# A hybrid encoder step with a mixture of experts on one core: the order of the loads around the last stage

## What is computed

```python
def finish_layer(x, p, o_attn, c, lp):
    ...
    x = x + mixed
    h = rms_norm(x, lp['g_ffn']).reshape(B * T, D)
    idx, wts = hier_route(h, lp['w_coarse'], lp['b_coarse'], lp['w_fine'], lp['b_fine'])
    x = x + moe_ffn(h, idx, wts, lp['w_e_gate'], lp['w_e_up'], lp['w_e_down']).reshape(B, T, D)
    gate = jax.nn.sigmoid(rms_norm(x, lp['g_ple']) @ lp['w_ple_gate'])
    return x + gate * (p @ lp['w_ple_proj'])
```

## Time and profile before

| | |
|---|---|
| median of three runs | 1413.82 us |
| profiled execution | 1412.76 us |
| its span in the profile | 1410.5 us |
| TensorE matmul, busy | 1283.0 us (91%) |
| VectorE, busy | 957.3 us (68%) |
| ScalarE, busy | 718.7 us (51%) |
| GpSimd, busy | 398.6 us (28%) |
| chain that ended last, by engine | PE 70%, DVE 11%, DMA 4%, issue 2% |
| last block's last scatter issued | 1255.82 us |
| first expert rows issued | 1260.67 us |
| last output issued | 1407.15 us |

### The profile page before, as it was taken

One profiled execution on the slowest core, in us unless ns is written; L12 is line 12 of the kernel. 1 busy time (PEld: TensorE's weight loads), 2 busy tenths in 40 slices (PEclk: granted clock), 3 DMA queues, 4 the chain that ended last, 5 costly groups with the idle time before them and its releaser, 6 DMA issues.

```text
span 1410.5 us, 18160 instructions
## 1 busy us (share of the span) xinstructions
PE 1283.0 (91%) x6337; PEld 1067.9 (76%) x6337; DVE 957.3 (68%) x940; ACT 718.7 (51%) x872; POOL 398.6 (28%) x399
## 2 busy tenths in 40 slices
PE   5999878889888799987999999999999999948887
PEld 4888867777676688845788888888888888837765
DVE  4233845655566332275999999999999999965443
ACT  4224034545453221241877777777777777742121
POOL 1000023443402000003344444444444444420000
PEclk9999989989858899988999999999999999978999
DMA  7521002000004321126899999999999999953332
GB/s 264 128 59 31 1 16 90 16 25 1 15 22 151 125 90 60 45 98 248 319 396 379 378 377 372 372 380 378 384 393 390 398 400 398 379 217 116 119 105 75
DMA packets 72223, 289.54 MB, mean 205 GB/s; under 512 B 24048, under 2 KB 26800, under 8 KB 46830
## 3 DMA queue, kind: packets, MB, share of 16 engines
q1 hardware_dynamic: 61950, 271.03, 51.3%
q0 software_dynamic: 10224, 17.85, 3.3%
HBM read 276.13 MB, written 32.17 MB: 219 GB/s over the span
## 4 chain that ended last, share of the span: by engine, by line
PE 70%; DVE 11%; DMA 4%; issue 2%; ACT 2%; POOL 1%; SPq 0%; POOLq 0%; DVEq 0%; ACTq 0%
PE ps L419 18%; PE ps L421 18%; PE ps L420 18%; PE ps L1729 3%; PE ps L1848 3%; DMA mem<-y_rows 2%; PE ps L1736 2%; PE ps L1875 1%; PE ps L1860 1%; PE ps L1996 1%; DVE whl L408 1%; PE ps L1909 1%; PE ps L1810 1%; PE ps L2015 1%; DVE mem L1334 1%
## 5 line engine op out<-in xcount | busy, mean ns | idle before, releaser
L408 DVE TENSOR_TENSOR whl<-mem,whl 128x2048 fp32r<-128x2048 f32 (+2 forms) x219 | 491.4, 2248 | 30.9 <-ACT whl L1114 20.8
L419 PE MATMUL ps<-whl,ahl 128*128 128x512 f32 x1120 | 449.0, 401 | 6.4 <-DVE ahl L408 3.4
L420 PE MATMUL ps<-whl,ahl 128*128 128x512 f32 x1120 | 437.0, 390 | 0.0
L421 PE MATMUL ps<-whl,ahl 128*128 128x512 f32 x1120 | 436.9, 390 | 0.0
L1114 ACT ACTIVATE whl<-mem 128x2048 fp32r<-128x2048 f32 x202 | 387.3, 1919 | 96.0 <-PE ps L421 96.0
L419 PEld LDWEIGHTS ps<-whl,ahl 128*128 128x128 f32 x1120 | 217.9, 195 | 47.8 <-issue 4.8
L421 PEld LDWEIGHTS ps<-whl,ahl 128*128 128x128 f32 x1120 | 215.4, 192 | 44.4
L420 PEld LDWEIGHTS ps<-whl,ahl 128*128 128x128 f32 x1120 | 216.8, 194 | 40.0
L819 POOL DMA_INDIRECT y_rows<-mem x35 | 94.0, 2686 | 293.3 <-DVE mem L1630 292.5
L716 POOL TENSOR_SCALAR mem<-mem 128x1 f32<-128x1 f32 (+2 forms) x68 | 16.3, 240 | 514.2 <-ACT mem L893 411.3
L893 ACT ACTIVATE mem<-mem 128x1024 bf16<-128x1024 f32 (+1 forms) x54 | 49.2, 912 | 215.8 <-DVE mem L1463 100.2
(11 more groups left out here) (231 smaller groups left out, 1451.5 us busy)
## 6 DMA issues: line engine op xcount, KB each, us to landing
mem<-in_w_e_up SPq DMA_DIRECT2D x66, 1024.0 KB, 7.3
mem<-in_w_e_gate SPq DMA_DIRECT2D x66, 1024.0 KB, 7.3
mem<-in_w_e_down SPq DMA_DIRECT2D x66, 1024.0 KB, 7.7
mem<-in_x_prompt SPq DMA_DIRECT2D x24, 512.0 KB, 3.5
mem<-y_rows SPq DMA_DIRECT2D x16, 512.0 KB, 6.0
mem<-in_w_in SPq DMA_DIRECT2D x4, 1024.0 KB, 11.5
mem<-in_w_out SPq DMA_DIRECT2D x4, 1024.0 KB, 5.1
h_rows<-mem SPq DMA_DIRECT2D x8, 512.0 KB, 2.6
```

The lines of the kernel that those rows point to most:

```text
L408: return which.tensor_tensor(out, full, hi.bitcast(F32), ALU.subtract)
L419: nc.tensor.matmul(out, act_hi, whl[:, 0, w_at], start=first, stop=False)
L420: nc.tensor.matmul(out, act_hi, whl[:, 1, w_at], start=False, stop=False)
L421: return nc.tensor.matmul(out, act_lo, whl[:, 0, w_at], start=False, stop=last)
```

## The change

The norm vector gets a place of its own, over constants that are used up once the slot tables are made, and SyncE issues its load right behind its loop over the experts. The loads of the expert rows become a function; tiles 0 and 1 are issued ahead of the loop, and turn t of the loop issues tile t+2 in front of the gate rows and the output. The first three pairs each wait for the one low part that frees their buffer, in place of all four; the wait for all four goes to VectorE, in front of its first add. In the two loops over the gate-weight chunks, the last block's scaling moves from in front of chunk 3 to in front of chunk 2.

```diff
@@ -206,7 +206,7 @@
-        gple = xs[0]
+        gple = mem[:, P:P + D]
@@ -647,6 +647,7 @@
             sp.wait_ge(s_tab, 1)
+            sp.dma_start(gple, a["g_ple"][0].partition_broadcast(P)).then_inc(s_gm, 16)
             spilled = sp.value_load(ebk[0:1, 0:1].bitcast(I32), min_val=0, max_val=NE - 1)
@@ -680,17 +681,21 @@
             sp.wait_ge(s_moe, 1)
-            sp.wait_ge(s_mlv, J_PLE + 4)
-
+
+            def load_experts(t):
+                r = rows_of(t)
+                if t >= 3:
+                    sp.wait_ge(s_x2, t - 2)
+                else:
+                    sp.wait_ge(s_mlv, J_PLE + t + 1)
+                for k in range(2):
+                    sp.dma_start(yb[t % 3][k][0:r], Y[k * TOKENS + t * P:k * TOKENS + t * P + r]).then_inc(s_y[t % 3], 16)
+
+            load_experts(0)
+            load_experts(1)
             for t in range(NT + 3):
-                if t < NT:
-                    r = rows_of(t)
-                    if t >= 3:
-                        sp.wait_ge(s_x2, t - 2)
-                    for k in range(2):
-                        sp.dma_start(yb[t % 3][k][0:r], Y[k * TOKENS + t * P:k * TOKENS + t * P + r]).then_inc(s_y[t % 3], 16)
-                    if t == 0:
-                        sp.dma_start(gple, a["g_ple"][0].partition_broadcast(P)).then_inc(s_gm, 16)
+                if t + 2 < NT:
+                    load_experts(t + 2)
                 if 3 <= t <= NT:
                     load_projected(t - 1)
@@ -1168,7 +1173,7 @@
             for c in range(4):
-                if c == 3:
+                if c == 2:
                     out_left(0, J_PLE, 16 * (NE + 2), 2 * NE + 4)
                 expert_hi(None, c, c, 16 * (NE + 2), J_PLE + c - 3)
@@ -1704,6 +1709,7 @@
+            dve.wait_ge(s_mlv, J_PLE + 4)
             add_experts(0)
             x2_norm(0)
```

## The result

The changed kernel takes 1389.21 us, median of four runs (1388.53 to 1389.54), against 1413.21 for the kernel before in the same measurements; the ratio is 0.9833, with a 95% interval of 0.9821 to 0.9845. The forecast was 1391, its range 1387.5 to 1396. The profiled execution took 1388.99 us (span 1386.8), 23.8 less than that of before.

A forecast was written before the change was run, and what follows sets the result against it. The last stage was taken as bound by expert-row loads issued too late, TensorE next. 1412.76 - 19.16 (rows) - 3.56 (head) = 1390.04, plus 1.06 from profiled execution to median, gave 1391; range 1387.5 to 1396.

The forecast's parts named there:

- Rows two tiles ahead: Last stage: rows issued ahead of the output of tile t-3 end the load wait; turns 16.33 to 11.805, -19.16 us.
- The new wait on s_x2: On SyncE, ahead of gate rows and outputs: already over when SyncE comes to it.
- The first rival: Last stage: half the mean wait for rows stays, turn 13.2, time 1401; chance 0.08.
- The ring of VectorE and ScalarE: Last stage: their own turn of 10.1 us is a floor, 1.7 us a turn remaining before it takes over.
- The norm vector: Head of the last stage: with its load off the chain, the first add starts 1.66 us sooner.
- The cover in the expert loop: Scatter has 3.1 us cover against the vector's 1.66; cost taken as 0. Rival, loop delayed: 1392.7 to 1394.5, chance 0.09.
- The scaling: Last block's end: right half scaled at about 1252.3 instead of 1254.2, -1.9 us.
- all behind it moves with it: Behind the scaling: scatter, its 3.54 us to landing, GpSimd's word and SyncE's issue all move by the same 1.9 us.
- the forecast of the head: Start of the last stage: moves forward by 1.66 + 1.9 = 3.56 us, or 2.3 to 4.9 by the skill's clock rule.
- the wait for the fourth low part: Moved from SyncE to VectorE: waits for VectorE's own earlier work, so costs nothing.
- rows still just in time: Rival: SyncE held at some wait, only the head's 3.56 remains, time 1410; chance 0.04.
- a clock that stays low: Rival: TensorE's clock stays at its lower level through the last stage, about 1449 us; chance 0.03.

The follow-up runs named there:

- after: The changed kernel with all parts of the change, against the kernel before: 1389.21 us, ratio 0.9833.
- one_ahead: Against the changed kernel, expert rows loaded one tile ahead of the other transfers in place of two: 1388.44 us, ratio 0.9823.
- after_again: The changed kernel as it is, measured again on the same chip as the version with matmuls in both TensorE gaps: 1389.32 us, ratio 0.9827.
- after_busy_vector: Against the changed kernel, one more unread low part on VectorE right behind the right half's scaling: 1391.09 us, ratio 0.9841.
- scale_and_waits: Against the kernel before, scaling in front of chunk 2 and the changed kernel's split low-part waits: 1410.09 us, ratio 0.9976.
- norm_only: Against the kernel before, only the norm vector's own place and its load behind SyncE's expert loop: 1412.22 us, ratio 0.9996.
- scale_only: Against the kernel before, only the last block's scaling moved in front of chunk 2: 1412.61 us, ratio 0.9996.
- before: The kernel before the change, unaltered: 1413.21 us in the same measurements as the changed kernel.
- rows_only: Of the change only the expert rows' load order and its waits; norm vector and scaling as in the kernel before: 1394.03 us, ratio 0.9867.
- the run in which it idled 0.29 us ahead of the first transposes and 1.93 behind them: Against the changed kernel, 68 unread matmuls on TensorE between the last block and last stage: 1386.91 us, ratio 0.9815.
- the other run: Against the changed kernel, GpSimd's early read of the further-block count, 67 unread matmuls before the first transposes and 7 behind: 1386.20 us, ratio 0.9808.
- the run with early reading and without the second set: Against the changed kernel, 68 unread matmuls before the last stage, and GpSimd reads the further-block count during its last scatter: 1386.28 us, ratio 0.9814.

## Why the prediction was right, and where not

**Rows two tiles ahead: right to the tenth.** 19.16 was forecast, 112.88 - 93.68 = 19.20 came, and the run with that part alone shows it as its own. What is late next is TensorE, as said: turns of 11.80 at a clock of 1.00. The new wait on s_x2 cost nothing that shows there. The first rival, rows hidden only in part, found no place: even one tile of lead hides them. The ring of VectorE and ScalarE, 10.1 by the forecast, never took over.

**The norm vector: 1.66 forecast.** From the scatter's landing to the first add it took 7.93 us before (1255.82 + 3.54 to 1267.29 of the chain) and 6.36 after (1257.39 to 1263.75): 1.57. The cover in the expert loop held, at a cost of nothing (573.8 us before and after). That the same 16 engines run all DMAs and interleave them, as the Trainium skill says ("DMA: Bandwidth & Descriptors", section "Issuing engines are not separate DMA queues"), agrees with the vector's own landing: 8.6 us in the loop, beside the weights, 5.75 before. But nothing on the path had so little slack. One reading was a little off: the first add for tile 1 came 5.99 us after that for tile 0, not 5.8, which changes nothing.

**The scaling: 1.9 forecast, 1.90 came, and its landing was mis-sized.** From the left scaling to the scatter's issue it took 3.54 us before and 1.64 after. The step "all behind it moves with it: scatter, its 3.54 us to landing" took the landing for a constant. It fell by 1.17, to 2.37, because GpSimd issued the scatter beside an idle VectorE; the runs with the scaling alone and with VectorE kept at work show that as the cause. This is most of what the forecast of the head lacked. The same part came out right by a step to which the forecast gave no weight: the wait for the fourth low part that goes from SyncE to VectorE was put at nothing. In the changed kernel it costs nothing, but without it the scaling gains only 0.9 of its 3.1, as the runs with and without the split wait show.

**The clock: inside its bounds, but it does not shift with the work.** The head was let shift as a whole, with 1.3 either way. From the first to the third transposes it took 17.27 before and 16.33 after: the rise came at about 1275.9, 6.0 us after the first transposes, where it came 8.1 after before. That is 0.94 of the gain. It looks like chance, since over the nine profiles of this study without added matmuls that piece is 16.26 to 17.75, with the rise 5.9 to 9.0 us after the first transposes. But counted from the last block's end (the last left scaling) the rise fell into three narrow groups, by how long the way to the first transposes is:

| runs | to first transposes | last left scaling to the clock's rise |
|---|---|---|
| after, one_ahead, after_again | 16.5 to 16.6 | 22.5 to 22.6 |
| after_busy_vector, scale_and_waits, norm_only | 17.8 to 19.7 | 25.8 to 25.9 |
| scale_only, before, rows_only | 20.3 to 21.3 | 29.2 to 29.4 |

The times are worked out from the mean clock of a stretch; for norm_only, with its scaling at 1251.82, the rise is at about 1277.7:

```profile
1276.00:1280.00 4.00, 4.00 (x16) 3.18 (x14) 3.65 (x3) 0.21 (x1) 0.05 (x1) 0.78 0.00 0
```

So the 0.94 came with the shorter head: the rise moved forward by 6.7 us, the first transposes by 4.6. A change of the head can gain or lose about 1 us more than itself in this way, as the run with VectorE kept at work did. What sets the three moments, no run here shows, and all kernels but the changed one have a single profile. The Trainium skill, "TensorE: Matmul & The Clock Gate", Part 1, has the moment vary from run to run; the two profiles of the changed kernel, 22.5 in both, do not show that.

**The sum.** Between the marks: 19.20 + 1.90 + 1.17 + 1.57 + 0.94 = 24.78, which is what was measured, against 22.72 forecast. The early stages took 1.1 of it back in the profiled pair, which leaves the 23.7 by which the span is shorter. So that the forecast's 1391 lies only 1.8 above the median is in part luck: the marks gained 2.06 more than was forecast, 1.17 of it in the scatter's landing, the term that was mis-sized, and 0.94 in the clock's rise, and the early stages hid half of that. The rest of the 1.8 is that the forecast added 1.06 from the execution to the median, where 0.22 came. The other rivals, rows still just in time and a clock that stays low, did not come.

## What to carry to other kernels

In a queue that one engine issues in order, put a load in front of the stores that wait for this turn's result: one turn of lead was as good as two here, and worth 19 of the 24 us. When a late step is moved forward, ask what its successor waits for besides, since a wait that joins several events can give the gain back, as the wait for four low parts did with the scaling. Small parts are read from marks within a profile; the runs' spread here, 0.2%, hides them. Where a stage starts at the clock's lower level, look at where the rise falls before a part's gain or loss is put down to the part alone.

## What the runs showed of the hardware that was not expected

An indirect DMA takes GpSimd longer to issue while VectorE splits a chunk. The last scatter's row was 0.99 us, with a landing after 2.4, in all eight kernels in which VectorE is idle beside it (the scaling in front of chunk 2 and nothing added behind it), and 2.17 us, with a landing after 3.5 to 3.6, in the four in which VectorE is at work (before, rows_only, norm_only, after_busy_vector). The Trainium skill, "GPSIMD Engine Reference", section "1. Specifications", says that GpSimd shares its SBUF interfaces with VectorE, with contention where VectorE's instruction has two SBUF inputs; the low part is such an instruction (it reads the chunk and its high part), and the trace agrees with its 1.18 us. No run sets an instruction with one such input beside the last scatter.

TensorE's clock, which was 1.00 while it worked through the gap, fell to a mean of 0.58 in the run in which it idled 0.29 us ahead of the first transposes and 1.93 behind them:

```profile
1272.00:1276.00 4.00, 3.67 (x10) 2.96 (x11) 3.06 (x4) 0.77 (x2) 0.74 (x2) 0.58 0.82 260
```

With the second gap filled, the same stretch of the other run (columns as before):

```profile
1272.00:1276.00 4.00, 4.00 (x18) 3.28 (x18) 3.03 (x4) 0.26 (x2) 0.75 (x2) 1.00 0.80 262
```

In the run with early reading and without the second set TensorE idled 1.74 us behind the first transposes and not ahead of them, and its clock stayed at 1.00 too. What of the idle time makes the clock fall is not shown.
